# Rotary part of the page scores in a hybrid mLSTM and MLA step: native products on two halves of the rows, in two banks

## The reference, cut to what matters

```
def mla_keys(c_kv, k_rope, w_uk, g_kn, g_kr):
    k_nope = jnp.einsum('...sc,chd->...shd', c_kv, w_uk)
    k_r = jnp.broadcast_to(k_rope[..., None, :], k_nope.shape[:-1] + (B_ROPE,))
    return qk_norm(k_nope, k_r, g_kn, g_kr)

def mla_attend(q, k, c_kv, mask, w_uv):
    s = jnp.einsum('bqhe,bkhe->bhqk', q, k).astype(jnp.float32) * ATTN_SCALE
    ...
```

## Time and profile before

| | |
|---|---|
| median of 3 runs | 2832.47 us |
| the profiled execution | 2833.95 us |
| its span, first to last instruction | 2832.0 us |
| PE (matmuls) busy | 2760.1 us, 97% |
| DVE busy | 1619.0 us, 57% |
| ACT busy | 1300.4 us, 46% |

### The profile page before, as it was taken

The page is one execution under the profiler, slowest core; times in us unless marked ns, Lnnn a source line. Parts: engine busy times, 40 slices in busy tenths (PEclk is TensorE's granted clock), DMA queues, the critical chain, the costliest instruction groups (busy, mean ns, idle before and its releaser), DMA issues. The chain is left out here.

```text
span 2832.0 us, 54134 instructions
## 1 busy us (share of the span) xinstructions
PE 2760.1 (97%) x19274; PEld 2618.9 (92%) x19274; DVE 1619.0 (57%) x2705; ACT 1300.4 (46%) x2333; POOL 403.3 (14%) x762
## 2 busy tenths in 40 slices
PE   8998799999999989999999999999999999999999
PEld 7865799999999978999999999999999999999999
DVE  4465776666566643555554444445777644677744
ACT  5536665555556543444453333344444433444432
POOL 0102333433334310000000000013000000000000
PEclk9999899999999999999999999999999999999999
DMA  6624112222222157565656555555555556555464
GB/s 193 236 68 106 36 33 62 63 51 56 53 63 50 52 199 209 166 199 169 198 154 197 163 165 165 167 176 174 164 164 163 149 165 185 164 168 162 138 186 126
DMA packets 696852, 393.54 MB, mean 139 GB/s; under 512 B 65240, under 2 KB 679330, under 8 KB 695720
## 3 DMA queue, kind: packets, MB, share of 16 engines
q1 hardware_dynamic: 684456, 378.64, 45.8%
q10 hardware_dynamic: 11824, 11.50, 1.2%
q0 software_dynamic: 368, 0.81, 0.1%
HBM read 368.13 MB, written 22.75 MB: 138 GB/s over the span
## 5 line engine op out<-in xcount | busy, mean ns | idle before, releaser
L288 DVE TENSOR_TENSOR w_lo_b<-stage,w_hi_b 128x2048 fp32r<-128x2048 f32 (+1 forms) x289 | 619.0, 2142 | 408.4 <-ACT w_hi_b L281 408.3
L281 ACT ACTIVATE w_hi_b<-stage 128x2048 fp32r<-128x2048 f32 (+1 forms) x289 | 517.9, 1792 | 583.5 <-PE bank L305 535.8
L300 PE MATMUL bank<-xnH,w_hi_b 128*128 128x288 f32 x2752 | 745.9, 298 | 2.9 <-PEq L191 2.4
L301 PE MATMUL bank<-xnL,w_hi_b 128*128 128x288 f32 x2752 | 740.7, 296 | 0.0
L300 PEld LDWEIGHTS bank<-xnH,w_hi_b 128*128 128x128 f32 x2752 | 517.0, 188 | 12.8 <-issue 11.5
L301 PEld LDWEIGHTS bank<-xnL,w_hi_b 128*128 128x128 f32 x2752 | 516.5, 188 | 0.3
L1671 PE MATMUL bank<-uk_all,lat 128*128 128x384 f32 (+1 forms) x1344 | 445.8, 332 | 22.8 <-DVE lat L2458 9.1
L1673 PE MATMUL bank<-uk_all,lat 128*128 128x384 f32 (+1 forms) x1344 | 436.1, 325 | 0.0
L305 PE MATMUL bank<-xnH,w_lo_b 128*128 128x288 f32 x2752 | 391.8, 295 | 0.0
L305 PEld LDWEIGHTS bank<-xnH,w_lo_b 128*128 128x128 f32 x2752 | 373.7, 188 | 0.0
L1671 PEld LDWEIGHTS bank<-uk_all,lat 128*128 128x128 f32 x1344 | 254.6, 189 | 42.6 <-issue 29.0
(11 more groups left out here) (520 smaller groups left out, 3757.3 us busy)
## 6 DMA issues: line engine op xcount, KB each, us to landing
stage<-in_w_in_dram SPq DMA_DIRECT2D x88, 1024.0 KB, 5.2
stage<-in_w_up_dram SPq DMA_DIRECT2D x88, 1024.0 KB, 5.4
stage<-in_w_down_dram SPq DMA_DIRECT2D x64, 704.0 KB, 4.6
raw<-in_cache_kv_latent_dram SPq DMA_DIRECT2D x256, 64.0 KB, 1.8
stage<-in_w_branch_a_dram SPq DMA_DIRECT2D x16, 1024.0 KB, 5.6
stage<-in_w_branch_b_dram SPq DMA_DIRECT2D x16, 1024.0 KB, 5.6
stage<-in_w_out_dram SPq DMA_DIRECT2D x16, 1024.0 KB, 5.6
vals<-in_cache_kv_latent_dram SPq DMA_DIRECT2D x60, 256.0 KB, 2.9
```

What stands on the lines that cost most here:

```text
L281: act.activation(h, a, ACT.Copy).then_inc(w_hi, 1)
L288: dve.tensor_tensor(lo, a, h.bitcast(F32), ALU.subtract).then_inc(w_lo, 1)
L300: pe.matmul(out, hi, xH(k), start=first and k == 0, stop=False)
L301: pe.matmul(out, hi, xL(k), start=False, stop=False)
```

## The change

The rotary products are made natively from `latT` itself, with no split. `rope`, `rope_high` and `rope_low` are gone, and with them `qHH` and `qLZ`; one query tile `qRR` takes their place, copied once from bank 7. The first page of a pair uses the first 64 partitions and writes to bank 7, the second uses the other 64 and writes to columns 384 to 447 of bank 2, which `p2` uses for its result in the columns ahead of those. `ropes` moves ahead of `p2`, and waits for the two transposes, for the copies of the last pair's rotary scores and for `sum11` of the group before. `p2` of the pair's second group waits for the copies of this pair's. VectorE copies the two pages' results with two instructions, and copies a batch's 64 query columns to `qrb` in `next_queries`. The first part of `new_scores` is one native product with 64 rows.

```diff
                     def p2(b, G):
                         need(pe, e_c11, upto(b, G - 1))
+                        if G % 3 == 1:
+                            pe.wait_ge(e_rope, pairs(b, G // 3))
                         product(b, G, bE, A12, B21, k_p[2], True)
                     def ropes(b, i):
-                        pe.wait_ge(f_rl, pairs(b, i))
+                        pe.wait_ge(f_t, b.of(NPG, 2 * i + 2))
                         need(pe, e_rope, pairs(b, i - 1))
-                        for x in range(2):
-                            out = bR[:, (2 * (i % 2) + x) * HQ:(2 * (i % 2) + x + 1) * HQ]
-                            pe.matmul(out, rope[:, x, :], qHH[:, bass.ds(b.of(), 1), :], start=True, stop=False)
-                            mm = pe.matmul(out, rope[:, x, :], qLZ[:, bass.ds(b.of(), 1), :], start=False, stop=True)
+                        need(pe, e_c11, upto(b, 3 * i - 1))
+                        if i == 0:
+                            pe.wait_ge(q_rope, b.of(1, 1))
+                        for x, out in enumerate((bR[:, i % 2 * HQ:(i % 2 + 1) * HQ], bE[:, BLK:BLK + HQ])):
+                            rows = slice(x * ROPE, (x + 1) * ROPE)
+                            mm = pe.matmul(out, latT[rows, x, KVL:], qrb[rows, b.mod(2), :], start=True, stop=True)
                         mm.then_inc(k_rope, 1)
                     def new_scores():
-                        pe.wait_ge(f_neg, 1)
                         pe.wait_ge(f_cnh, 1)
                         ps = bV[0:N_S]
-                        pe.matmul(ps, krrS[:, 0:N_S], qHH[:].rearrange("p b q -> p (b q)"), start=True, stop=False)
-                        pe.matmul(ps, krrS[:, 0:N_S], qLZ[:].rearrange("p b q -> p (b q)"), start=False, stop=False)
+                        pe.matmul(ps, krT[:], qRR[0:ROPE].rearrange("p b q -> p (b q)"), start=True, stop=False)
...
                             p1(b, G)
-                            p2(b, G)
                             if pos == 0:
                                 ropes(b, i)
+                            p2(b, G)
...
-                        at = 2 * (i % 2) * HQ
-                        dve.tensor_copy(sc[:, b.mod(2), 2 * i:2 * i + 2, :], bR[:, at:at + 2 * HQ].rearrange("p (j q) -> p j q", j=2)).then_inc(e_rope, 1)
+                        dve.tensor_copy(sc[:, b.mod(2), 2 * i, :], bR[:, i % 2 * HQ:(i % 2 + 1) * HQ])
+                        dve.tensor_copy(sc[:, b.mod(2), 2 * i + 1, :], bE[:, BLK:BLK + HQ]).then_inc(e_rope, 1)
...
                         dve.tensor_copy(q_raw[:], qlat_pages[:, :, bass.ds(b.of(), 1), :].rearrange("p k o q -> p k (o q)")).then_inc(q_tmp, 1)
+                        dve.tensor_copy(qrb[:, b.mod(2), :], qRR[:, bass.ds(b.of(), 1), :].rearrange("p o q -> p (o q)")).then_inc(q_rope, 1)
```

More of the change, by code:

```diff
@@ L314, in build @@
         c_new = sb(kept, "c_new", [N_S, KVL])
-        qHH = sb(kept, "qHH", [P, NB, BH * S_S], F32R)
-        qLZ = sb(kept, "qLZ", [P, NB, BH * S_S], F32R)
+        qRR = sb(kept, "qRR", [P, NB, BH * S_S])
         qlat = sb(kept, "qlat", [P, LC, NB, BH, S_S])
@@ L540, in build @@
             v_mm, v_ev = sem("vv_mm"), sem("vv_ev")
-            qd_mm, qd_z, qd_hi, qd_lo = (sem("qd_" + x) for x in ("mm", "z", "hi", "lo"))
+            qd_mm, qd_ev = (sem("qd_" + x) for x in ("mm", "ev"))
             e_s, e_sc, e_sm, e_mx, e_ex, e_rc, e_nm, e_t, e_tev, e_o, e_oev = (
@@ L872, in _ @@
                         if h == 7:
-                            pe.wait_ge(qd_lo, 1)
+                            pe.wait_ge(qd_ev, 1)
                         if h >= 3 and h % 2 and h < BH + 2:
@@ L1123, in _ @@
                             act.wait_ge(qd_mm, 1)
-                            act.activation(qHH[:].rearrange("p b q -> p (b q)"), bank[7][:], ACT.Copy).then_inc(qd_hi, 1)
+                            act.activation(qRR[:].rearrange("p b q -> p (b q)"), bank[7][:], ACT.Copy).then_inc(qd_ev, 1)
                         if h >= 6 and h % 4 == 2:
@@ L1216, in _ @@
                     dve.memset(krg[:], 0.0).then_inc(kg_z, 1)
-                    dve.memset(qLZ[:].rearrange("p b q -> p (b q)").bitcast(F32), 0.0).then_inc(qd_z, 1)
                     dve.wait_ge(x_rt, 1)
@@ L1337, in _ @@
                             dve.wait_ge(r_ss, 1)
[L1338 to L1342, removed]
                         if h == 5:
@@ L1492, in build @@
             cnT = nc.alloc_sbuf_tensor_at("cnT", [P, LC, N_S], F32, offset=STAGE + 4 * (AT_END + 4 * P))
-            krrS = nc.alloc_sbuf_tensor_at("krrS", [P, P], F32R, offset=STAGE + 4 * (AT_END + 5 * P))
+            krT = nc.alloc_sbuf_tensor_at("krT", [ROPE, N_S], F32, offset=STAGE + 4 * (AT_END + 5 * P))
             latT = sb(ph, "latT", [P, 2, KVL + P])
-            rope = sb(ph, "rope", [P, 2, P], F32R)
             cb = sb(ph, "cb", [P, 4, BLK])
@@ L1499, in build @@
             s1, u4 = su[:, 0], su[:, 1]
+            qrb = sb(ph, "qrb", [P, 2, HQ])
             rows_r = sb(ph, "rows_r", [P, 4, ROPE])
@@ L1533, in build @@
             uk_hi, uk_lo = (sem("uk_" + x) for x in ("hi", "lo"))
-            f_t, f_sum4, a_hi, a_lo, f_rh, f_rl, f_ss = (sem("p_" + x) for x in ("t", "sum", "hi", "lo", "rh", "rl", "ss"))
+            f_t, f_sum4, a_hi, a_lo, f_ss = (sem("p_" + x) for x in ("t", "sum", "hi", "lo", "ss"))
             rr_in = [sem(f"rr_in{n}") for n in range(4)]
@@ L1541, in build @@
             e_c11, e_c21, e_c22, e_r11, e_r12, e_r21, e_r22, e_sc12, e_sc, e_rope = (sem("t_" + x) for x in ("c11", "c21", "c22", "r11", "r12", "r21", "r22", "sc12", "sc", "rope"))
-            f_kz, f_mz, f_cr, f_cn, f_cnh = (sem("f_" + x) for x in ("kz", "mz", "cr", "cn", "cnh"))
-            (f_neg, f_sn, f_sn1, f_scn, f_ra, f_rr, f_rc, f_sev, f_snc, f_m8, f_mxp,
+            f_mz, f_cr, f_cn, f_cnh = (sem("f_" + x) for x in ("mz", "cr", "cn", "cnh"))
+            (f_sn, f_sn1, f_scn, f_ra, f_rr, f_rc, f_sev, f_snc, f_m8, f_mxp,
              f_mt, f_mc, f_mw, f_mb, f_sub, f_ex, f_p8, f_ps, f_sum, f_o, f_rs, f_ol, f_ot, f_oev, f_h, f_hev) = (
-                sem("f_" + x) for x in ("neg", "sn", "sn1", "scn", "ra", "rr", "rc", "sev", "snc",
+                sem("f_" + x) for x in ("sn", "sn1", "scn", "ra", "rr", "rc", "sev", "snc",
                                         "m8", "mxp", "mt", "mc", "mw", "mb", "sub", "ex", "p8", "ps", "sum", "o", "rs", "ol", "ot", "oev", "h", "hev"))
@@ L1926, in split @@
                         act.activation(lat[:, op, 0, :], latents(op), ACT.Copy).then_inc(a_hi, 1)
[L1928 to L1934, removed]
                     def rope_squares(b, i):
@@ L2015, in batch @@
                                     split(b, i, A22)
-                            if pos == 1 and not (last and i == PR - 1):
-                                rope_high(b, i + 1)
                             if post and G == 2:
@@ L2044, in _ @@
                     split(At(0), 0, A12)
-                    rope_high(At(0), 0)
                     uk_high(0, 2)
@@ L2055, in _ @@
                     act.wait_ge(f_cn, 1)
-                    act.wait_ge(f_kz, 1)
-                    act.activation(krrS[:, 0:N_S], bM[:, 0:N_S], ACT.Copy)
+                    act.activation(krT[:], bM[0:ROPE, 0:N_S], ACT.Copy)
                     act.activation(cnT[:], bM[:, N_S:(LC + 1) * N_S].rearrange("p (k r) -> p k r", k=LC), ACT.Copy).then_inc(f_cnh, 1)
@@ L2153, in batch @@
                                 pool.wait_ge(q_part, (b + 1).of(3, 3))
-                    pool.memset(krrS[:].bitcast(F32), 0.0).then_inc(f_kz, 1)
                     query_low(At(0), slice(0, 2))
@@ L2223, in turn @@
                         need(dve, a_lo, b.of(7 * PR, 7 * i))
-                        need(dve, f_rl, b.of(PR, i))
+                        need(dve, k_rope, b.of(PR, i))
                         for x in range(2):
@@ L2228, in turn @@
                             dve.transpose(latT[:, x, :].rearrange("p (m b j) -> p m b j", b=4, j=QD), raw[:, j % RAW, :].rearrange("p (b m i) -> p m b i", b=4, i=QD)).then_inc(f_t, 1)
[L2230 to L2236, removed]
                     def next_queries(b):
@@ L2355, in batch @@
                                     uk_low(G + 1, x)
-                            if pos == 2 and more:
-                                rope_low(b, i + 1)
                             if post and G == 1:
@@ L2467, in _ @@
                     first_sum(1)
-                    rope_low(At(0), 0)
                     first_sum(2)
```

4 lines of the change are left out of this document (1 added, 3 removed).

## The result

The changed kernel takes 2836.44 us (median of 20 runs) where the kernel before takes 2832.53 on the same chip: ratio 1.0013, 95% interval 1.0007 to 1.0018, so 3.9 us more with an interval of 2.0 to 5.1. The forecast was +3.2 us. A second series of runs gave 1.0015 (1.0006 to 1.0024). The move is clear of noise and under the 0.2% that the prediction called the limit of one measurement.

The account below looks back on a forecast made before the run. TensorE's order was taken to bound the batches, DVE and ACT the start. Pairs +3.0 us after 0.8 swallowed, start +0.2, together +3.2 on 2832.47: 2835.7 us, range 2829 to 2842.

Parts of the forecast that it names:

- What bounds the kernel: Inside the batches TensorE's own order sets the time; relieving DVE or ACT brings nothing there, save at waits.
- The price of the pair: Rotary products of two pages: 0.57 us after for 0.45 before, 3.8 us more for 32 pairs.
- sign of 0.87 us where 0.30 would do: PE's timeline, last product of `p1` to second of `p2`: 0.87 us expected at all pairs.
- Side by side: The two pages' products, on different rows and banks, overlap on PE; the second adds only 0.01 us.
- The rival without a price for the mode: The pair costs 0.22 us, -7.4 us for 32; kernel at 2825.3 us; chance 0.06.
- The swallowed 0.8 us: PE's seven waits for `copy_s1` each shrink by 0.12 us, taking 0.8 us off the pairs' cost.
- The order and the waits: `ropes` ahead of `p2`, and `p2` waiting for the score copies: costed at nothing for PE.
- its third rival: DVE is late for `sum21`, so PE waits: +4.2 us on top of the forecast, 2839.9 us; chance 0.12.
- The start: Start of the page stage: -0.4 us on DVE, +0.6 for `new_scores`, together +0.2 us.
- DVE part of the term: At the start `rope_low` and the `krrS` fill leave DVE's chain, the `qrb` copy enters: -0.4 us.
- DVE in time: In the group with `less`, 0.72 us of new delay fits DVE's 0.91 us wait before `sum21`, by 0.2 us.

Follow-up runs that it names:

- full rows with early zeros: The changed kernel with all 128 rows in each rotary product, the query's second half zeroed by DVE at the very beginning: 2833.69 us, ratio 1.0004.
- the extra product: The kernel before with one unused native product more in each pair, ahead of the split ones: 2846.33 us with 64 rows, 2837.01 us with 128.
- the last experiment: The kernel before with each page's two split products made as one of 128 moving columns, halves added by DVE: 2826.26 us, ratio 0.9976.
- The order alone: The kernel before with only the rotary products moved ahead of `p2`: 2832.90 us, ratio 1.0001.
- both kernels with full rows: The changed kernel with 128-row rotary products, zeros set by POOL at the page stage's start (2836.43 us) or by DVE at the very beginning (2833.69 us).

## Why the prediction was right, point by point

- *What bounds the kernel: right.* 20 us less of DVE and 10 us less of ACT brought nothing in the batches. The full rows with early zeros show it best: DVE and ACT relieved in the same way (469.4 and 420.5 us busy in the stage, for 488.6 and 430.3), the pair at 0.44 us as before, and the time is that of before (1.0004, 0.9994 to 1.0013). Only PE's own time moved the kernel.
- *The price of the pair: right.* 0.57 us was forecast from `spread`'s row, 0.56 to 0.57 came, in 31 of 32 pairs; the first one runs at the lower clock level. That the price is the change of rows is shown by three pairs of kernels: 64 against 128 rows in the pair (0.12 us), the pair made twice (0.22 us for as much work again), and the extra product (0.34 us). The three fit together: side by side, four passes take 0.22 us for 0.45, the way there and back takes 0.34, and 0.45 - 0.22 + 0.34 = 0.57. Two readings of `spread` were weaker than the number taken from them. Its weights waited for DVE by the profile, as this row shows, so a part of its 0.56 us could have been DVE's:

```profile
527.23 0.29 PEld L1743 LDWEIGHTS bank<-cst,mxw 64*128 64x128 f32 x2 [0.24 <-DVE mxw L2273]
```

  The extra product with 64 rows waits for nobody and costs 0.56 us too (0.22 with 128 rows and 0.34), so it wasn't. And the 0.28 us from the first full product to its successor is no sign of the change of rows: behind the four full-row products of before it is 0.25 us (645.95 to 646.20). The prediction's sign of 0.87 us where 0.30 would do came as 0.83 for 0.27, since both steps there are of 288 columns; the pair's share is the same.
- *Side by side: right.* The eight records of the mLSTM stage were the right witness, though with 32 rows. With the same half for both pages the pair costs 0.22 us more. The Trainium skill's doubled speed for a contracted dimension of 64 ("TensorEngine Tiling (Array Packing)", Theoretical Speedup) is there between the two halves (0.22 us for four passes that take 0.44 one after the other) and is lost at their edges. The rival without a price for the mode left out that shorter rotary products lengthen the seven waits; by its own 0.23 us that is 1.6 us, and 1.5 came in the last experiment.
- *The swallowed 0.8 us: right*, 3.3 to 2.5 us. One more wait of PE, in the first batch, swallowed 0.1.
- *The order and the waits: right but for 0.3 us.* The order alone costs nothing, and none of PE's waits names the copies. But the prediction put all new waits at nothing, and those for `copy_u4` cost 0.3 us (four batches at 0.08). It had itself named growing waits for ACT as the sign of its third rival. The same 0.3 us is in both kernels with full rows and not in the order alone, so it comes with the native form, the two copies or their waits, and not with the 64 rows; which of them is open.
- *The start: wrong in sign.* Forecast +0.2 us. Product by product, the changed kernel stands 0.35 us ahead of before at the end of PE's long wait (298.31 us), 0.3 and 0.2 us ahead behind `new_scores` in its two profiles, and 0.7 and 0.6 us ahead at 323 us. The DVE part of the term (-0.4 us) came as forecast. What failed is `new_scores`: 1.6 us for its native product, on the guess that most of it would run at the lower level. It took 1.00 us and 1.08, as the two split ones of before had (0.99), with 0.13 more ahead of it:

```profile
301.49 1.07 PE L1727 MATMUL bank<-qRR,krT 64*32 64x512 f32 x2
302.49 3.62 PE L1729 MATMUL bank<-qlat,cnT 128*32 128x512 f32 x8
```

  The granted clock from 301.6 to 303.0 us is 1.00 here and 0.50 in before, so it ran at the level of 2.4 GHz where the split ones had run at 1.2. That is luck as much as the change: of the four kernels that still have the query tiles and `new_scores` of before, the extra product with 128 rows and the last experiment stand 0.5 and 0.4 us ahead of before at 323 us as well, the order alone and the extra product with 64 rows within 0.1 us of it.
- *DVE in time: right, with more spare than I thought.* The timeline of DVE in the group with `less` shows it, against the earlier trace rows:

```profile
530.86 0.46 DVE L2158 TENSOR_TENSOR cb<-bank,su 128x288 f32<-128x288 f32 x1 [0.52 <-PE bank L1667]
531.23 0.21 DVE L2199 COPY sc_s<-bank 128x64 f32<-128x64 f32 x1
531.36 0.21 DVE L2200 COPY sc_s<-bank 128x64 f32<-128x64 f32 x1
...
534.62 0.56 DVE L2172 TENSOR_TENSOR cb<-bank,su 128x384 f32<-128x384 f32 x1 [0.78 <-issue]
```

The wait ahead of `sum21` shrank from 0.91 to 0.78 us, not to 0.2. In before DVE had idled 0.26 us for ACT a little ahead of `less` in the same group, at 532.56 us; that is gone, and the later `sum11` used it first.

The sum by these numbers: -0.7 at the start, 31 x 0.115 = +3.6 for the pairs, -0.9 swallowed, +0.3 at the waits for `copy_u4`, +2.3 us. The measured 3.9 us has an interval from 2.0 to 5.1, so the sum lies in its lower part. The same holds for the full rows with early zeros (-0.1 by the sum, +0.8 measured, -1.7 to +3.7). So the price of the pair was right for its reason, but that +3.2 came so near to 3.9 is in part luck: the start was 0.9 us better than its term, and some 1 to 2 us are not in the sum. They may lie outside the page stage. Behind the stage's last product the six profiles with the new query tile last 1790.5 to 1793.4 us, the five with the old one 1790.0 to 1791.4, 1.2 us less in the mean, with ranges that overlap. What makes the difference stays open: no step of the change stands there, and the places of the stretches at the lower clock level differ from one execution to the next.

## What to carry to other kernels

Before cutting a product down to half the rows, look what stands on either side of it: among full-row products the way there and back costs more (0.34 us here) than a few short products, and the halves pay only when several pairs of products stay in that mode: here one pair costs 0.57 us for 0.45 with full rows, and two in a row cost 0.79, for which two with full rows would take some 0.9 (an estimate from 2 x 0.45). Neighbours that are in the mode too should save the way as well; no run here shows that. A short product with 128 columns of weights costs 0.11 us here, the step from load to load, whether 64 or 128 columns move. So put more moving columns behind one load before removing work from DVE or ACT. And price a change of mode by the nearest row that has it, from start to start over the neighbours, never by the busy time of the product.

## What the runs showed of the hardware that was not expected

- A split product (`fp32r`) of 128 moving columns costs as much as one of 64: 0.11 us (0.23 for two, where four of 64 cost 0.45).
- Two DVE copies of 128 x 64 from two banks, 0.21 us each, start 0.13 us apart, so the second costs 0.13.
- POOL's first small subtraction behind a memset of 64 partitions took 2.75 us, once, where it took 0.77 before. It was seen in one profile, and its cause is not known.
- One stretch of 3.4 us at the lower clock level inside the page stage (granted clock 0.50 from 671.8 to 675.1 us) cost about 1.4 us, a third of the effect that was to be measured. It shows in the distance between equal products of two traces, and hardly in the page.
